# A two-layer encoder trunk with routed experts: last expert pair in pieces, first z block of the second layer in fp32, x turned from a plain copy

## What is computed

```python
for l in range(2):
    z = x @ w_in[l]                        # (256 x 1024) @ (1024 x 6656)
    qa, ka, va, ub, qc, kc, vc, ga, gb, gc = split(z)
    ya, yb, yc = attention(qa, ka, va), pooling(ub), differential_attention(qc, kc, vc)
    merged = sigmoid(ga)*(ya @ w_branch_a) + sigmoid(gb)*(yb @ w_branch_b) + sigmoid(gc)*(yc @ w_branch_c)
    x = layer_norm(alpha * x + merged @ w_out, ln1_g[l], ln1_b[l])
    # 64 experts, 8 of them for a token, and one shared expert
    y = shared_expert(x) + routed_experts(x, top8(x))   # silu(x@gate) * (x@up) @ down
    x = layer_norm(alpha * x + y, ln2_g[l], ln2_b[l])
```

## Time and profile before

| | |
|---|---|
| median of 3 runs | 1467.1 us (1466.84 to 1468.67) |
| profiled execution, its own time | 1469.81 us |
| span of that execution | 1468.0 us |
| PE busy | 1429.4 us, 97% of the span |
| DVE, ACT busy | 550.1 us, 465.4 us |
| moved by DMA | 497.76 MB, mean 339 GB/s |
| mean granted TensorE clock | 0.993 |

### The profile page before, as it was taken

The page is one execution under the profiler, slowest core; times in us unless marked ns, Lnnn a source line. Parts: engine busy times, 40 slices in busy tenths (PEclk is TensorE's granted clock), DMA queues, the critical chain, the costliest instruction groups (busy, mean ns, idle before and its releaser), DMA issues.

```text
span 1468.0 us, 23807 instructions
## 1 busy us (share of the span) xinstructions
PE 1429.4 (97%) x10104; PEld 868.8 (59%) x10104; DVE 550.1 (37%) x882; ACT 465.4 (32%) x745; POOL 32.9 (2%) x30
## 2 busy tenths in 40 slices
PE   9999999999999999989899999999999999999995
PEld 8999998544444444434289999984434334333441
DVE  4577756321221221211365778571122221221223
ACT  5565444222122221112246744432222222221212
POOL 0021000000000000000001110000000000000000
PEclk9999999999999999999999999999999999999998
DMA  9663588599999999999665445776999999999994
GB/s 309 203 210 129 196 315 358 217 429 423 426 425 426 425 425 425 422 424 425 273 243 177 157 173 226 296 315 265 424 426 425 424 426 425 426 424 425 424 426 152
DMA packets 80436, 497.76 MB, mean 339 GB/s; under 512 B 6160, under 2 KB 11536, under 8 KB 47312
## 3 DMA queue, kind: packets, MB, share of 16 engines
q1 hardware_dynamic: 78048, 492.61, 82.8%
q10 hardware_dynamic: 2288, 3.67, 0.8%
HBM read 493.90 MB, written 1.05 MB: 337 GB/s over the span
## 4 chain that ended last, share of the span: by engine, by line
PE 78%; DMA 14%; DVE 3%; SPq 2%; ACT 2%; issue 1%; DVEq 0%
PE bank L1713 28%; PE bank L1538 14%; PE bank L1741 12%; DMA arena<-in_expert_w_gate_up 10%; PE bank L1658 6%; PE bank L1687 4%; PE bank L1603 3%; PE bank L1493 3%; PE bank L1431 2%; DMA ring_w<-in_w_out 2%; PE bank L1727 1%; ACT w_hi L717 1%; PE bank L1679 1%; DMA ring_w<-in_w_in 1%; PE bank L1576 1%
## 5 line engine op out<-in xcount | busy, mean ns | idle before, releaser
L1538 PE MATMUL bank<-x_hi,w_hi 128*128 128x256 f32 x704 | 200.9, 285 | 0.5 <-ACT arena L783 0.5
L945 DVE TENSOR_TENSOR w_lo<-ring_w,w_hi 128x2048 fp32r<-128x2048 f32 x71 | 162.4, 2289 | 101.9 <-ACT w_hi L717 101.7
L1538 PE MATMUL bank<-x_hi,w_lo 128*128 128x256 f32 x704 | 199.2, 283 | 0.0
L1538 PE MATMUL bank<-x_lo,w_hi 128*128 128x256 f32 x704 | 199.2, 283 | 0.0
L1713 PE MATMUL bank<-arena,xe_odd 128*64 128x512 f32 x768 | 174.9, 609 | 11.4 <-DMA arena<-in_expert_w_gate_up 10.7
L1348 DVE SCALAR_TENSOR_TENSOR y_lo<-bank,slot_info,y_hi 128x512 fp32r<-128x512 f32 x128 | 96.0, 750 | 208.4 <-ACT y_hi L861 208.4
L1713 PE MATMUL bank<-arena,xe_even 128*64 128x512 f32 x768 | 170.1, 595 | 3.0 <-DMA arena<-in_expert_w_gate_up 2.7
L1336 DVE TENSOR_TENSOR hid<-hid,bank 128x256 f32<-128x256 f32 x64 | 27.0, 421 | 385.8 <-ACT hid L847 385.8
L847 ACT ACTIVATE hid<-bank 128x256 f32<-128x256 f32 x64 | 24.6, 385 | 427.9 <-PE bank L1713 427.9
L861 ACT ACTIVATE y_hi<-bank,slot_info 128x512 fp32r<-128x512 f32 x128 | 88.1, 688 | 226.7 <-PE bank L1741 226.7
L717 ACT CAST w_hi<-ring_w 128x2048 fp32r<-128x2048 f32 x71 | 135.1, 1904 | 57.8 <-PE bank L1603 30.5
(11 more groups left out here) (214 smaller groups left out, 1788.0 us busy)
## 6 DMA issues: line engine op xcount, KB each, us to landing
arena<-in_expert_w_gate_up SPq DMA_DIRECT2D x48, 4096.0 KB, 22.0
gu_c<-in_expert_w_gate_up SPq DMA_DIRECT2D x16, 4096.0 KB, 23.3
ring_w<-in_w_in SPq DMA_DIRECT2D x25, 2048.0 KB, 9.0
arena<-in_expert_w_down SPq DMA_DIRECT2D x24, 2048.0 KB, 21.5
dn_a<-in_expert_w_down SPq DMA_DIRECT2D x24, 2048.0 KB, 19.6
dn_c<-in_expert_w_down SPq DMA_DIRECT2D x16, 2048.0 KB, 21.4
ring_w<-in_w_out SPq DMA_DIRECT2D x4, 2048.0 KB, 11.0
ring_w<-in_w_branch_a SPq DMA_DIRECT2D x2, 2048.0 KB, 8.6
```

The costliest lines, as they stand in the source:

```text
L945: v.tensor_tensor(chunk_part(w_lo, n), chunk_in(n), chunk_part(w_hi, n).bitcast(F32), ALU.subtract).then_inc(w_lo_ready, 1)
L1538: ins = mm(b[:, S * c:S * c + S], lhs, rhs, start=(k == 0 and a + w == 0), stop=(k == KD - 1 and a == 1))
```

## The change

It has four parts.

1. The last pair (31) of each layer is loaded in pieces: the up weights as four DMAs of 1 MB, each with two of the eight contraction steps, the down weights as two halves of the output columns, each in two DMAs. PE waits for each piece where it first reads it.
2. The first z block of layer 1 is loaded behind the last pair's weights and the norm vectors. It is no longer split: PE reads it from `ring_w` in fp32, and x from a plain copy `x_first` that ACT makes of each transpose. x_hi and x_lo are made from `x_first` afterwards, all four before chunk 2 is split. The block's slot is reloaded when PE has finished z task 1.
3. The vectors of the second norm are issued by SP behind the last weights, no longer by ACT at pair 30.
4. In layer 0 x is also loaded in natural order into `x_rows`, two DMAs of 128 partitions, and turned from there. `x_tok` is loaded later, behind block 5, for the residual. `in_order` and the four small copies of va and vc per task go in layer 0.

```diff
             for t in range(TT):
-                for h in range(TT):
-                    sp.dma_start(x_tok[CHUNK * h:CHUNK * h + CHUNK, t, :],
-                                 x[0, P * h + CHUNK * t:P * h + CHUNK * t + CHUNK, :]).then_inc(x_in[t], 16)
+                sp.dma_start(x_rows[:, t, :], x[0, P * t:P * t + P, :]).then_inc(x_in[t], 16)
...
-                if bl >= 0:
+                if bl > 0 and before == 0:
+
+                    wait_task(sp, bl, ("z", 1, 0))
+                elif bl >= 0:
...
+            def load_last(l, used):
+
+                weights = expert_w_gate_up[l, NE - 2:NE].rearrange("e (p k) n -> p e k n", k=KD)
+                sp.wait_ge(up_done, used)
+                sp.sem_inc(loads_cleared, 1)
+                for c in range(LAST_UP):
+                    ks = slice(KD // LAST_UP * c, KD // LAST_UP * (c + 1))
+                    sp.dma_start(gu[1][:, :, ks], weights[:, :, ks]).then_inc(last_up_in[c], 16)
+                weights = expert_w_down[l, NE - 2:NE].rearrange("e (p k) n -> p e k n", k=KF)
+                sp.wait_ge(y_done, 2 * used)
+                sp.sem_inc(loads_cleared, 1)
+                for h in range(2):
+                    cols = slice(512 * h, 512 * h + 512)
+                    for e in range(2):
+                        sp.dma_start(dn[1][:, e, :, cols], weights[:, e, :, cols]).then_inc(last_down_in[h], 16)
+
+            def load_tokens():
+
+                for t in range(TT):
+                    for h in range(TT):
+                        sp.dma_start(x_tok[CHUNK * h:CHUNK * h + CHUNK, t, :],
+                                     x[0, P * h + CHUNK * t:P * h + CHUNK * t + CHUNK, :]).then_inc(tok_in, 16)
...
-                if l + 1 < L:
-                    sp.wait_ge(y_done, 2 * (2 * start + SHORT_FROM - 2))
-                    load_block(l + 1, 0)
-
-                with sp.Fori(0, short_steps(more)) as i:
+                with sp.Fori(0, short_steps(more) - 1) as i:
                     pair = 2 * ((i + SHORT_FROM // 2) & (HALVES - 1))
                     for u in range(2):
                         load_after(l, u, pair + u, 2 * (i + start) + SHORT_FROM + u - 1)
+                last = 2 * (start + more * HALVES + HALVES) - 1
+                load_after(l, 0, PAIRS - 2, last - 2)
+                load_last(l, last - 1)
+                load_ln(sp, l, 1)
 
                 if l + 1 < L:
-
+                    load_block(l + 1, 0)
                     sp.wait_ge(acc_done, 2 * TT * (l + 1))
                     load_block(l + 1, 1)
...
                         if j == 3:
-                            for u in range(0 if l == 0 else 2, WBUFS):
+                            for u in range(4 if l else 0):
+                                x_high(l, u)
+                            for u in range(2 if l else 0, WBUFS):
                                 split_high(l, u)
...
-                    if last and not odd and l + 1 < L:
-
-                        split_high(l + 1, 0)
-                        split_high(l + 1, 1)
-                    if last and not odd:
-
-                        load_ln(act, l, 1)
...
-                    if u == 0 and l + 1 < L:
-                        for c in range(2):
-                            split_low(l + 1, c)
...
+            def unsplit(l, u, j):
+
+
+                if u == 0:
+                    wait_evac(pe, l, ("xt", 0, j))
+                t = j // 2
+                for k in range(KW * (j % 2), KW * (j % 2) + KW):
+                    ins = mm(bank(l, ("z", u, 0))[:, S * t:S * t + S], x_first[:, k, P * t:P * t + P],
+                             slot_of_block(BLOCK_OF_Z[0], KD)[:, k, S * u:S * u + S], start=(k == 0), stop=(k == KD - 1))
+                return ins
...
-                        for t in range(TT) if l == 0 else (1,):
-                            ins = first_tile(l, i, t)
+                        if l == 0:
+                            for t in range(TT):
+                                ins = first_tile(l, i, t)
+                        else:
+                            for j in range(2, 4):
+                                ins = unsplit(l, i, j)
...
+                        if last and k % (KD // LAST_UP) == 0:
+                            pe.wait_ge(last_up_in[k // (KD // LAST_UP)], 16 * (l + 1))
...
+                        if last:
+                            pe.wait_ge(last_down_in[h], 32 * (l + 1))
```

More of the change, by code:

```diff
@@ L80 @@
 FIRST_UP = 14
+LAST_UP = 4
 def unit(i):
@@ L351, in build @@
         dn_in = [sem(f"dn_in{n}") for n in range(3)]
+        last_up_in = [sem(f"last_up_in{c}") for c in range(LAST_UP)]
+        last_down_in = [sem(f"last_down_in{h}") for h in range(2)]
         out_done = sem("out_done")
@@ L761, in _ @@
                             ins = nc.scalar.activation(sig[:, 2 * v:2 * v + 2, :], two, ACT.Sigmoid)
+                        elif name in ("va", "vc") and l == 0:
+                            ins = nc.scalar.copy((va if name == "va" else vc)[:, :, S * half:S * half + S], two)
                         elif name in ("va", "vc"):
@@ L1187, in _ @@
                         elif j == 3:
+                            for u in range(4):
+                                x_low(l, u)
+                            dve.sem_inc(w_lo_ready, 2)
                             split_low(l, 2)
@@ L1462, in keep_warm @@
                     mm(b[:, 0:rhs.shape[1]], lhs, rhs, start=True, stop=True)
-            def ahead(l, u, half, passes):
-                n = CHUNK_AT["z", 0, u]
-                b = bank(l, ("z", u, 0))
-                for a, w in passes:
-                    for k in range(KW * half, KW * half + KW):
-                        mm(b[:, 0:S], (x_hi, x_lo)[a][:, k, 0:P], chunk_part((w_hi, w_lo)[w], n)[:, k, :],
-                           start=(k == 0 and a + w == 0), stop=(k == KD - 1 and a == 1))
+            def unsplit(l, u, j):
[6 more added lines that the diff above has]
+                return ins
             start = shorts = 0
@@ L1695, in combine, with pair_step @@
                     return ins
-                def pair_step(n, g, odd, step, slot, loads, following=None, first=False):
+                def pair_step(n, g, odd, step, slot, loads, following=None, first=False, last=False):
                     bank_up, bank_other = (bank_even, bank_odd)[::-1 if odd else 1]
                     early, late = gathers_in(step, g.width, following)
-                    pe.wait_ge(gu_in[slot], 16 * loads)
+                    if not last:
+                        pe.wait_ge(gu_in[slot], 16 * loads)
                     if not first:
```

87 lines of the change are left out of this document (52 added, 35 removed).

## The result

| | before | changed |
|---|---|---|
| median in the same comparison | 1467.88 us (1466.84 to 1471.12, 4 runs) | 1459.0 us (1458.87 to 1459.84, 4 runs) |
| profiled execution, its own time | 1469.81 us | 1459.04 us |
| span of that execution | 1468.0 us | 1457.2 us |
| PE, DVE, ACT busy | 1429.4, 550.1, 465.4 us | 1426.3, 545.8, 458.7 us |
| mean granted TensorE clock | 0.993 | 0.997 |

The ratio is 0.9934, 95% interval 0.9922 to 0.9947: the changed kernel is faster by some 9 us. The forecast was 1455.8 us, with a range of 1453 to 1460. The sign and the mechanism hold, and the time lies in the range, 3.2 us above the forecast.

The account below looks back on a forecast made before the run. The prediction took PE as the bound outside the expert stages and DMA as their pacer by 0.3 us a pair. 9.6 + 4.5 + 1.2 - 3.0 - 1.0 = 11.3 us off 1467.1 gave 1455.8 us, range 1453 to 1460.

Parts of the forecast that it names:

- Layer 0's tail: Last expert pairs of layer 0: z block moved and last pair in pieces end up 31 9.6 us earlier.
- Layer 1's tail: Last expert pair of layer 1: loading in pieces ends up 31 at 1443.1 instead of 1447.6, 4.5 us gained.
- the carrying of an earlier arrival through a stage that DMA paces: Expert stages: the 1.2 us gained at the kernel's start was counted whole in the sum.
- The issue cost of 0.37 us a piece: SP's queue at the last pair: each extra issue costs 0.37 us while 10 us are queued.
- The boundary: Between layers 0 and 1: fp32 z block loses 3.0 us, a new wait for block 2 loses 1.0.
- Rival (a): Layer boundary: block 2 takes 9.5 us, a wait over 2 us drops the clock; 1459.7 us, chance 0.15.
- the quick one of the two values: Layer boundary: block 2 needs 9.5 us to land, or 7.7 as quicker loads did.
- the prediction's order of work: PE at the layer boundary: transposes, ACT's copies and fp32 matmuls in turn, ending at 755.0 instead of 752.1.
- The start: First layer: x in two DMAs of 128 partitions moves at 400 instead of 240 GB/s, 1.2 us gained.
- the term "clock": Up 31 with the clock staying up: 7.1 us, where layer 0's took 8.78; counted inside the tails' gains.
- the base: Whole kernel: terms taken off 1467.1 us, the median of the runs shown, beside a profiled 1469.81.
- the norm vectors' share: Pair 31's load: norm vectors on the second queue make it 0.6 us later in layer 0, 0.9 in layer 1.

Follow-up runs that it names:

- z_old_place: The changed kernel with z block 0 loaded between pairs 25 and 26 again, still unsplit; median 1465.95 us, ratio 0.9980.
- reordered: The changed kernel with block 2 loaded in halves, chunk 2 split earlier and the first tile's fp32 products dealt out between ACT's copies; 1456.26 us, ratio 0.9917.

## Why the prediction was right, and where it was off

**Layer 0's tail, forecast 9.6.** Measured 9.37, and the steps as they were told: the wait at pair 26 went to 0.23, up 31 started at 707.28 without a wait (708.4 less the start's lead) and ran 7.09 us, the down part was there. z_old_place alone moves the 5.66 us wait in and out. The 9.37 are net of 0.6 us of the start's lead that were lost at pair 24 (1.35 to 0.75), which the prediction didn't count.

**Layer 1's tail, forecast 4.5.** Measured 4.00. The 2.9 of the wait and the 1.7 of the clock are there; 0.6 us of lead were lost on the way, in short waits for weights between pairs 23 and 30. The term that was off is the carrying of an earlier arrival through a stage that DMA paces: it was taken as whole, and 6.27 of 6.87 us arrive at pair 30, since PE comes to wait for weights. The issue cost of 0.37 us a piece was off too, without effect.

**The boundary, forecast 3.0 and 1.0 lost.** Measured 2.73 and 1.11, in the place named (before z4, 0.68 us of visible wait). Rival (a), a wait long enough to drop the clock, didn't come: block 2 landed 7.75 us after its issue, the quick one of the two values that the prediction had, which is luck. With that value the prediction's own sum gives a wait of 0.4 us; the 1.0 taken was a value between, and it fits because z1 ends 0.35 us behind the start of z2 (744.48 and 744.13) and the steps up to z4 have small gaps. The three short waits for ACT's copies lie in the prediction's order of work; that two of them can be filled, reordered showed.

**The start, forecast 1.2.** Measured 1.33 in the profile, inside an uncertainty of 1 to 2 us that one profile has there (1.5 by the executions without GpSimd's wait), so the agreement to 0.1 us is luck. The DMA moved 380 GB/s in 4 to 6 us where it moved 240, and the first product came at 9.67, 2.09 earlier.

**The sum and the median.** The sum of the terms was 11.3, and the spans differ by 10.8. Yet the medians differ by less, and the forecast from the median missed by 3.2 us. Three steps make that up, as a matter of arithmetic. 0.5 is the sum. 1.2 is that the terms were read from an execution of 1469.81 us, which lay that much above the median of 56 executions, 1468.63. A likely reason is that it has both falls of the clock, where four of six waits had one: the term "clock" was counted at 3.4 us, where by that count it is worth some 2.3 in a median. That is an estimate from six waits; scatter of the start or of GpSimd's wait could be in the 1.2 as well. And 1.5 is the base, 1467.1 us as the median of three runs, 1.5 below that of the 56. The last two add up: a saving read from a long execution was taken off a low base. The prediction noted the two times side by side and did not correct for it; taken off 1468.63 with the clock at two thirds the sum would be 10.2 and the time 1458.4.

**Parts that don't add.** Against the kernel before, the pieces alone bring 6.9 us and all but the pieces (whole_last) 6.6 (1468.39 to 1461.81), and the whole change 9.9, not 13.5. A part that both take away is counted twice: the fall of the clock after pair 31's wait, some 2.3 us, and the 1.5 us by which the wait shrank in whole_last, which fits the norm vectors' share as predicted (0.6 and 0.9). No kernel here moves the norm vectors alone with the last pair whole, so that share is argued.

## What to carry to other kernels

Here a transfer that stood in a saturated queue cost its whole length at the end of the stage. Moved behind the last use, it costs only what it is late there, but what the move asks for must be counted too: the fp32 product and block 2's later load gave 3.7 to 4 of the 5.2 to 6 us back. Cutting the last load into pieces that are used as they land saves the wait for the rest of it. When a term is a stall of an engine whose clock can fall, read several executions before counting the fall, and take terms and base from the same kind of execution. Where a chain of small copies feeds an engine, deal the work out so that each copy has other work ahead of it: no wait at the boundary was over 0.8 us, and reordered, which fills two of them and loads block 2 earlier, is 2.7 us faster.

## What the runs showed of the hardware

The clock after a wait: waits of 1.75, 1.84, 1.87 and 2.82 us were followed by products at 2.4 GHz, waits of 2.18, 2.23, 2.51, 2.82 and 2.84 us by a stretch at 1.2 GHz, which cost 1.7 us at the up product and 1.4 us in z2 (the 2.51). The six waits of 5.65 to 5.73 us before pair 26 all had it, and pair 26's up product took 8.48 to 8.94 us for 7.09. The same 2.82 us went both ways, so the length of a wait alone doesn't foretell it. The Trainium skill, page "TensorE: Matmul & The Clock Gate", section "Part 1: The HAM clock gate", says of the rise of the clock under sustained matmuls that its moment varies from run to run; these rows show the same of its fall.

With x in loads of 128 partitions the DMA moved 380 GB/s in 4 to 6 us, where with loads of 64 it moved 240, a factor of 1.6. The Trainium skill, page "SBUF — State Buffer", section "Door 1: The DMA port swizzle", would have a factor of 2, since 64 partitions in one half reach 8 of 16 ports. The window of the changed kernel also holds the first weights, so it doesn't measure the rule's number alone.

Queued pieces of 1 MB and of 512 KB cost no fixed time one after the other; the rate fell by 4% with the last pair in 8 DMAs and by 7% with 12 (422, 404 and 392 GB/s). The Trainium skill, page "DMA: Bandwidth & Descriptors", section "Anatomy of one DMA", gives 2.0 us for each DMA, and gives it for DMAs that GpSimd issues, where these are SP's, which the prediction doesn't say. Whatever the fixed part is here, in a full queue it lies beside the transfers of the others.
